# Both down-projection tiles of an expert in one transfer: neurons dealt by eights, up columns read in runs of 8

## The chip, the cores and the metric

The kernel runs on one core of one Trainium2 chip. The metric is the device time of one execution in microseconds, the median of three runs; a profiled execution has a time of its own and a trace.

## What is computed

One decoder layer on 512 tokens of width 1024: a mixing sub-layer (attention, not touched here), then a mixture of experts with 32 experts, of which each token takes four. The part that matters:

```
def clamped_swiglu(u):
    x_glu, x_lin = u[..., ::2], u[..., 1::2]
    x_glu = jnp.minimum(x_glu, SWIGLU_LIMIT)
    x_lin = jnp.clip(x_lin, -SWIGLU_LIMIT, SWIGLU_LIMIT)
    return x_glu * jax.nn.sigmoid(SWIGLU_ALPHA * x_glu) * (x_lin + 1)
...
    up = lax.ragged_dot(xs, w_up, group_sizes) + b_up[e_sorted]
    down = lax.ragged_dot(clamped_swiglu(up), w_down, group_sizes) + b_down[e_sorted]
    out = jnp.zeros_like(hf).at[tok].add(down * g_sorted[:, None].astype(down.dtype))
```

An expert's `w_up` is 1024 x 2048 float32 (8 MB), its `w_down` 1024 x 1024 (4 MB). Column 2n and 2n+1 of `w_up` are the two inputs of neuron n, and row n of `w_down` is its output. Any order of the 1024 neurons gives the same sum.

## The kernel before

After the attention (up to about 415 us) a router sorts the tokens by expert into chunks of 32 slots; in this input there are 80 chunks. An expert's weights stand in SBUF as six tiles of 2 MB: tiles 0 to 3 are `w_up` (by its rows), tiles 4 and 5 are `w_down`. There are two sets of six, `par` 1 and 0, so that one expert can be loaded while another is used. PE works through 42 parts, each a run of chunks of one expert; four parts make a cycle, with three experts loaded in each of the ten cycles (`N_CYC`), 30 in all. The first two experts are loaded ahead.

For a chunk, PE (`part`) goes through the up tiles in `UP_ORDER` with the 32 tokens as weights: for each tile and each half `y` of the neurons, 2 x 4 products of 256 columns (L2016), four side by side in the four column strips of the array (`out_of(y, g)`). A float32 product stands as two instructions in the trace, so a chunk has 128 of L2016. DVE and ACT make the gated activations of half `y` and DVE turns them in 32x32 blocks (`actT[:, y]`). Then PE waits for `actT_ready[y]` and for `tile_in[par][4 + y]` and makes the down products of tile 4 + y (L2036, 32 instructions a half). At the end of each half `tile_used[4 + y]` rises. ACT scales the result (L970), and POOL scatters it with an adding indirect DMA into `token_sums`; another indirect DMA of POOL (L710) gathers the rows of a later chunk.

Which neuron meets which partition is set by the turn in blocks: partition 32g+r of `actT[:, y]` holds four neurons. Before, `w_dn` deals them as n = 512y + 4p + k, so tile 4 is the upper half of the matrix and tile 5 the lower, each with 16 KB in one piece for a partition.

All weight transfers are issued by SP, in one queue and in program order. `load_expert` waits for each tile until the last chunk that reads it is done, then issues: tile 0, tile 1, tiles 2 and 3 in one transfer of 4 MB (32 KB for a partition), tile 4, tile 5.

```
                sp.wait_ge(tile_used[2], used)
                sp.wait_ge(tile_used[3], used)
...
                for n in (4, 5):
                    sp.wait_ge(tile_used[n], used)
                    if not par and n == 4:
                        load_bias(slot, e)
                    load_tile(n, par, e)
```

The biases are split by POOL into three bfloat16 parts early in the program (L641, L644), written to HBM, and read back per expert (`load_bias`); PE adds them with small selection matrices `bsel` (L2024, L2030).

Of the kernel before, what the change touches and what calls it, by code (L numbers as in the profile page):

```python
# [7 lines left out]
ALU = mybir.AluOpType  # L8
# [7 lines left out]
P = 128  # L16
SEQ = 512
D = 1024
# [84 lines left out]
def hybrid_layer(nc, a, out):  # L103
# [6 lines left out]
    w_up2 = a["w_up"][0].rearrange("e (p z j) n -> z p e (j n)", p=P, z=2)  # L110
    w_dn = a["w_down"][0].rearrange("e (y p g) n -> y p e (g n)", p=P, y=2)
    consts = nc.inline_tensor(shape_constants(), name="shape_table").ap()
# [10 lines left out]
    with ExitStack() as ctx:  # L123
# [120 lines left out]
        def const(at, n):  # L244
            return cf[:, at - C_KEEP:at - C_KEEP + n]
# [184 lines left out]
        TILE_H, TILE_2 = 0, 8  # L430
        BCONST, ONES = 17, 2
        GATE_PARTS = (4, 5, 10, 11)
# [7 lines left out]
        def _(sp):  # L440
# [80 lines left out]
            def load_bias(b4, e):  # L521
                src = bias_d[bass.ds(e, 1)] if not isinstance(e, int) else bias_d[e:e + 1]
                sp.dma_start(biasw[0:36, b4, :], src.rearrange("e r n -> (e r) n")).then_inc(biasw_in[b4], 16)
# [62 lines left out]
            def load_expert(q, done, par, slot):  # L586

                e = of_place(ORD, q, 0, N_EXP - 1)
                used = of_place(FIRST, done, 1, MAX_CH)
                if par:  # L590
                    load_bias(slot, e)
                for n in (0, 1):
# [3 lines that stand above are left out]
                sp.wait_ge(tile_used[3], used)  # L596
                sp.dma_start(take((6 * (1 - par) + 2) * TILE, 2 * TILE), w_up2[1][:, bass.ds(e, 1)].rearrange("p e n -> p (e n)"))\
                  .then_inc(tile_in[par][3], 16)
                for n in (4, 5):
                    sp.wait_ge(tile_used[n], used)  # L600
                    if not par and n == 4:
                        load_bias(slot, e)
                    load_tile(n, par, e)

# [23 lines left out]
        def _(pool):  # L628
# [8 lines left out]
            pool.wait_ge(bias_in, 32)  # L637
            pool.wait_ge(ev_dve, 4)
            for part in range(3):
                split = bias_b[:, part, :]  # L640
                pool.tensor_copy(split, bias_f).then_inc(bias_split, 1)  # L641
                pool.wait_ge(bias_split, 2 * part + 1)
                if part < 2:
                    pool.tensor_tensor(bias_f, bias_f, split, ALU.subtract).then_inc(bias_split, 1)  # L644
                    pool.wait_ge(bias_split, 2 * part + 2)
            for part in range(3):
# [17 lines left out]
            for i in range(NT):  # L664
                pool.memset(tokb[:, i, 1:2], -4.0 * P * (NT - 1 - i)).then_inc(bconst, 1)
            pool.tensor_scalar(bsel.rearrange("p y g s -> p (y g) s"), bc(const(C_I96, 12), 2, SLOTS),
                               const(C_THIRD, 1), None, ALU.is_equal).then_inc(bconst, 1)
            pool.wait_ge(bias_out, 96)
# [94 lines left out]
        def _(act_e):  # L763
# [32 lines left out]
            def proj_evac(n):  # L796
                for i in range(NT):
# [14 lines left out]
                    elif n == 1:  # L812
                        if i == 0:
                            act_e.wait_ge(bias_split, 5)
                        for dup in range(2):
# [743 lines left out]
        def _(pe):  # L1559
# [432 lines left out]
            ins.then_inc(gate_ps, 1)  # L1992
            def part(q, par, slot, loads, bias_loads, with_third):

# [7 lines left out]
                with pe.Fori(0, chunks) as j:  # L2002
                    c = first + j

                    def out_of(bank, g):
                        return ps[SLOTS * g:SLOTS * (g + 1), bank, 0:256]

                    pe.wait_ge(xgT_ready, c + 1)
                    for y, n in UP_ORDER:
                        if y == 0:  # L2010
                            place = 3 if n == 2 and with_third else n
                            pe.wait_ge(tile_in[par][place], loads + (32 if (par, place) == (0, 3) else 0))
                        for k in range(2):
                            for g in range(4):
                                at = y * D + 256 * g
                                ins = pe.matmul(out_of(y, g), xgT[:, 2 * n + k, :],  # L2016
                                                tiles[par][n][:, k, at:at + 256],
                                                start=(n == 0 and k == 0), stop=False)
                        if y:
                            ins.then_inc(tile_used[n], 1)  # L2020
                        if n == 3:
                            pe.wait_ge(biasw_in[slot], bias_loads)
                            for g in range(4):
                                ins = pe.matmul(out_of(y, g), bsel[:, y, g, :], biasw[:, slot, :],  # L2024
                                                start=False, stop=True)
                            ins.then_inc(up_ps[y], 1)
# [4 lines left out]
                    for y in range(2):  # L2031
                        pe.wait_ge(actT_ready[y], c + 1)
                        pe.wait_ge(tile_in[par][4 + y], loads)
                        for k in range(4):
# [47 lines left out]
```

## Time and profile before

| what | value |
|---|---|
| time, median of 3 runs (lowest, highest) | 1415.01 us (1412.33, 1415.05) |
| profiled execution: its time, its span | 1411.59 us, 1409.7 us |
| mean granted clock of PE | 0.985 |
| PE busy (matmuls) | 1284.7 us, 91% |
| DVE, ACT, POOL busy | 44%, 25%, 22% |
| DMA queue of SP (q1): 466.61 MB | 80.1% of 16 engines' time |
| chain that ended last | PE 61%, DMA 30%, of which 24% transfers of `in_w_down` |
| up products (L2016), down products (L2036) | 582.3 us, 302.5 us busy |

The first 415 us hold the attention and the router, the 970 us behind them the experts, and the last 20 us the sum of the token rows and the final norm. In the stretch of the experts both PE and the DMA engines are busy nearly always; a share of DMA of 1.00 means that all 16 engines have work throughout. In the timeline a value in brackets is how long the engine sat idle before the instruction, and what ended it. In the chain, a line "DMA" runs from the issue of a transfer to its landing, which includes its time behind others in the queue.

### The profile page before, as it was taken

To read this page: it belongs to the slowest core of one execution; us is meant where nothing else is said; L and a number is where in the kernel's file an instruction comes from. 1 tells how busy PE (TensorE), PEld (TensorE's weight loads), DVE (VectorE), ACT (ScalarE), POOL (GpSimd) and SP (SyncE) were. 2 spreads that over 40 slices of the span, in tenths; PEclk is the share of its full clock that TensorE was granted. 3 is DMA by queue.
4 is the path that set the end of the run, shared out by engine and by line. 5 is a ranking of instruction groups with operands and counts; after the bars stand their busy time and mean duration, and the time that the engine had idled before them with its cause. 6 is when DMAs were issued, how large, how long until landed. Compare 5 with 4: busy or idle time off the path is not lost.

```text
span 1409.7 us, 45665 instructions
## 1 busy us (share of the span) xinstructions
PE 1284.7 (91%) x18509; PEld 754.1 (53%) x18510; DVE 623.8 (44%) x1737; ACT 345.9 (25%) x868; POOL 312.0 (22%) x421
## 2 busy tenths in 40 slices
PE   6999998999989999978989967799999999998994
PEld 3464455665555555544555534455555555555552
DVE  2578537884563333432333323233333433332345
ACT  2110016783232222211222211122222222221222
POOL 0400003553002222211222211122222222222222
PEclk9999999999999999999999989999999999999998
DMA  9877404005699999999999999999989989999998
GB/s 352 279 263 276 167 0 180 2 2 215 249 386 379 400 415 420 425 424 418 419 420 410 418 427 428 421 415 412 420 339 421 388 343 400 421 425 429 409 424 319
DMA packets 66540, 484.96 MB, mean 344 GB/s; under 512 B 9770, under 2 KB 16738, under 8 KB 45764
## 3 DMA queue, kind: packets, MB, share of 16 engines
q1 hardware_dynamic: 58052, 466.61, 80.1%
q0 software_dynamic: 8144, 17.78, 4.8%
q8 instruction: 27, 0.44, 0.1%
q14 instruction: 13, 0.11, 0.0%
q10 hardware_dynamic: 304, 0.02, 0.0%
HBM read 468.83 MB, written 19.93 MB: 347 GB/s over the span
## 4 chain that ended last, share of the span: by engine, by line
PE 61%; DMA 30%; DVE 4%; issue 3%; ACT 1%; SPq 1%; DVEq 0%; POOL 0%; POOLq 0%; ACTq 0%
DMA arena<-in_w_down 24%; PE ps L2016 23%; PE ps L2036 13%; PE ps L1677 9%; PE ps L1909 4%; DMA token_sums<-arena 3%; PE ps L1805 2%; PE ps L1776 2%; PE ps L1839 2%; DMA arena<-in_w_in 1%; PE ps L1644 1%; DMA arena<-xn_rows,arena 1%; DMA arena<-token_numbers 1%; PE ps L2024 1%; ACT arena L970 0%
## 5 line engine op out<-in xcount | busy, mean ns | idle before, releaser
L2016 PE MATMUL ps<-arena 128*32 128x256 f32 x10240 | 582.3, 381 | 44.7 <-issue 29.0
L2016 PEld LDWEIGHTS ps<-arena 128*32 128x32 f32 x10240 | 341.3, 111 | 262.3 <-issue 52.1
L2036 PE MATMUL ps<-arena 128*32 128x256 f32 x5120 | 302.5, 387 | 36.8 <-DMA arena<-in_w_down 35.4
L1495 DVE TENSOR_SCALAR arena<-ps 128x128 f32<-128x128 f32 x160 | 46.6, 291 | 565.7 <-PE ps L2024 560.4
L2036 PEld LDWEIGHTS ps<-arena 128*32 128x32 f32 x5120 | 155.9, 111 | 160.6 <-issue 45.8
L970 ACT ACTIVATE arena<-ps,arena 32x256 f32<-32x256 f32 x316 | 147.4, 466 | 380.2 <-DMA token_sums<-arena 239.5
L710 POOL DMA_INDIRECT arena<-xn_rows,arena x82 | 85.5, 1042 | 409.6 <-DVE arena L1456 266.5
L702 POOL DMA_INDIRECT token_sums<-arena x80 | 110.9, 1386 | 221.3 <-ACT arena L970 218.4
L961 ACT ACTIVATE arena<-arena 128x128 f32<-128x128 f32 x160 | 49.5, 310 | 387.6 <-DVE arena L1495 387.5
L1677 PE MATMUL ps<-arena 128*128 128x512 f32 (+1 forms) x320 | 127.7, 555 | 0.0
L1677 PEld LDWEIGHTS ps<-arena 128*128 128x128 f32 x320 | 60.1, 190 | 60.8 <-issue 57.7
L685 POOL TENSOR_SCALAR arena<-arena 128x128 f32<-128x128 f32 (+3 forms) x48 | 51.7, 1083 | 121.3 <-DVE arena L1262 109.4
L1503 DVE STREAM_TRANSPOSE arena<-arena 128x128 f32<-128x128 f32 x160 | 67.2, 420 | 5.5
L1456 DVE STREAM_TRANSPOSE arena<-arena 128x256 f32<-128x256 f32 x81 | 52.7, 651 | 18.5 <-DMA arena<-xn_rows,arena 15.9
L852 ACT ACTIVATE arena<-arena 128x128 f32<-128x128 f32 (+3 forms) x96 | 52.9, 552 | 27.9 <-DVE arena L1240 27.8
L1909 PE MATMUL ps<-arena 128*128 128x512 f32 x128 | 56.4, 595 | 0.0
L1498 DVE SCALAR_TENSOR_TENSOR arena<-arena 128x128 f32<-128x128 f32 x160 | 46.9, 293 | 20.4
L750 POOL COPY arena<-arena 128x1 int32 x79 | 21.7, 275 | 149.5 <-DMA arena<-xn_rows,arena 149.2
L1501 DVE TENSOR_TENSOR arena<-arena 128x128 f32<-128x128 f32 x160 | 46.7, 292 | 6.3 <-ACT arena L961 0.8
L2024 PE MATMUL ps<-arena 128*32 128x256 bf16 x640 | 47.8, 274 | 0.0
L1055 DVE SCALAR_TENSOR_TENSOR arena<-arena 128x512 f32<-128x512 f32 x56 | 46.0, 821 | 2.0
L1240 DVE CUSTOM_DVE_ANT_0 arena<-ps,arena 128x128 f32<-128x128 f32 (+3 forms) x96 | 42.0, 484 | 6.6 <-PE ps L1776 6.6
(335 smaller groups left out, 951.3 us busy)
## 6 DMA issues: line engine op xcount, KB each, us to landing
arena<-in_w_up SPq DMA_DIRECT2D x67, 2048.0 KB, 14.0
arena<-in_w_down SPq DMA_DIRECT2D x64, 2048.0 KB, 28.5
arena<-in_w_up SPq DMA_DIRECT2D x30, 4096.0 KB, 26.6
arena<-in_w_ada SPq DMA_DIRECT2D x11, 2048.0 KB, 12.0
arena<-in_w_in SPq DMA_DIRECT2D x5, 2048.0 KB, 9.8
arena<-in_w_o SPq DMA_DIRECT2D x2, 2048.0 KB, 10.6
arena<-in_x SPq DMA_DIRECT2D x4, 512.0 KB, 5.0
arena<-in_w_ada SPq DMA_DIRECT2D x2, 1024.0 KB, 11.9
```

The lines of the kernel that those rows point to most:

```text
L685: ins = pool.tensor_scalar(pb, pb, scl[:, u % 4, 2 * n + 1:2 * n + 2], None, ALU.mult)
L702: pool.indirect_dma_start(sums, bass.IndirectOffsetOnAxis(idxs, 0), rows, None, bounds_check=SEQ - 1, oob_is_err=False, compute_op=ALU.add ...
L710: pool.indirect_dma_start(xg_in, None, xn2_d, bass.IndirectOffsetOnAxis(rows, 0), bounds_check=4 * SEQ - 1, oob_is_err=False).then_inc(gat ...
L852: ins = act_e.activation(pb, pb, ACT.Exp, scale=-1.0, bias=negm[:, n:n + 1], accum_out=lsum[:, n:n + 1])
L970: ins = act_e.activation(ybuf[:, 256 * g:256 * (g + 1)], ps[rows, 5, 0:256], ACT.Copy, scale=gate_all[rows, bass.ds(c, 1)])
L1456: v.transpose(turned, rows).then_inc(xg_turned, 1)
L1503: v.transpose(actT[:, y], act[:, y].rearrange("p (r g) -> p g r", g=4)).then_inc(actT_ready[y], 1)
L1677: ins = pe.matmul(ps[:, pj_bank(t), 0:width], hT[:, kt, i * P:(i + 1) * P], w[:, kt, :], start=(kt == 0), stop=(kt == KT - 1))
L1909: ins = pe.matmul(ps[:, t % 2 * 2 + grp, :], oT[:, kt, i * P:(i + 1) * P], wo[n][:, kt, :], start=(j == 0), stop=(j == 3))
L2016: ins = pe.matmul(out_of(y, g), xgT[:, 2 * n + k, :], tiles[par][n][:, k, at:at + 256], start=(n == 0 and k == 0), stop=False)
L2024: ins = pe.matmul(out_of(y, g), bsel[:, y, g, :], biasw[:, slot, :], start=False, stop=True)
L2036: ins = pe.matmul(out_of(5, g), actT[:, y, k, :], tiles[par][4 + y][:, k, 256 * g:256 * (g + 1)], start=False, stop=(y == 1 and k == 3))
```

## The change

Neurons are dealt as n = 8p + 4y + k. A partition's eight rows of `w_down` then lie side by side, 32 KB in one piece, and inside the loop tiles 4 and 5 come by one transfer of 4 MB, issued when both are free and announced on `tile_in[par][5]`; PE waits for that semaphore ahead of each of the two halves. The two transfers ahead of the loop stay two. In return the up columns of half y in strip g are no longer 256 neighbours but 32 runs of 8 out of 512 columns, and the biases of the up columns are split in the same order: what was one operation of 768 columns on POOL is now two of 256 in runs of 8 and one of 256. The selection matrix `bsel` is made by three operations, not one.

```
-    w_dn = a["w_down"][0].rearrange("e (y p g) n -> y p e (g n)", p=P, y=2)
+    w_dn = a["w_down"][0].rearrange("e (p y g) n -> y p e (g n)", p=P, y=2)
+    w_dn2 = a["w_down"][0].rearrange("e (p j) n -> p e (j n)", p=P)
...
-        BCONST, ONES = 17, 2
+        BCONST, ONES = 19, 2
...
-                for n in (4, 5):
-                    sp.wait_ge(tile_used[n], used)
-                    if not par and n == 4:
-                        load_bias(slot, e)
-                    load_tile(n, par, e)
+                sp.wait_ge(tile_used[4], used)
+                sp.wait_ge(tile_used[5], used)
+                if not par:
+                    load_bias(slot, e)
+                sp.dma_start(take((6 * (1 - par) + 4) * TILE, 2 * TILE), w_dn2[:, bass.ds(e, 1)].rearrange("p e n -> p (e n)"))\
+                  .then_inc(tile_in[par][5], 16)
...
+            up_f, down_f = bias_f[:, 0:512].rearrange("p (r y c) -> p y r c", y=2, c=8), bias_f[:, 512:768]
             for part in range(3):
-                split = bias_b[:, part, :]
-                pool.tensor_copy(split, bias_f).then_inc(bias_split, 1)
-                pool.wait_ge(bias_split, 2 * part + 1)
+                up_b = bias_b[:, part, 0:512].rearrange("p (y r c) -> p y r c", y=2, c=8)
+                down_b = bias_b[:, part, 512:768]
+                for y in range(2):
+                    pool.tensor_copy(up_b[:, y], up_f[:, y]).then_inc(bias_split, 1)
+                pool.tensor_copy(down_b, down_f).then_inc(bias_split, 1)
+                pool.wait_ge(bias_split, 6 * part + 3)
                 if part < 2:
-                    pool.tensor_tensor(bias_f, bias_f, split, ALU.subtract).then_inc(bias_split, 1)
-                    pool.wait_ge(bias_split, 2 * part + 2)
+                    for y in range(2):
+                        pool.tensor_tensor(up_f[:, y], up_f[:, y], up_b[:, y], ALU.subtract).then_inc(bias_split, 1)
+                    pool.tensor_tensor(down_f, down_f, down_b, ALU.subtract).then_inc(bias_split, 1)
+                    pool.wait_ge(bias_split, 6 * part + 6)
...
-                            act_e.wait_ge(bias_split, 5)
+                            act_e.wait_ge(bias_split, 15)
...
-            def part(q, par, slot, loads, bias_loads, with_third):
+            def part(q, par, slot, loads, bias_loads, in_pairs):
...
+                    def up_columns(row, y, g):
+                        return row[:, 512 * g:512 * g + 512].rearrange("p (r y c) -> p y r c", y=2, c=8)[:, y]
+
...
-                                at = y * D + 256 * g
-                                ins = pe.matmul(out_of(y, g), xgT[:, 2 * n + k, :],
-                                                tiles[par][n][:, k, at:at + 256],
+                                ins = pe.matmul(out_of(y, g), xgT[:, 2 * n + k, :], up_columns(tiles[par][n][:, k], y, g),
...
-                        pe.wait_ge(tile_in[par][4 + y], loads)
+                        pe.wait_ge(tile_in[par][5 if in_pairs else 4 + y], loads)
```

SP, one `load_expert` of `par` 1 inside the loop, before (an ISA row is a wait or a register instruction; `tile_used4` is the semaphore for tile 4):

```order
L518 ISA [waits tile_used0]
L518 DMA arena<-in_w_up 128x4096
L518 ISA [waits tile_used1]
L518 DMA arena<-in_w_up 128x4096
L597 ISA [waits tile_used3,tile_used2]
L597 DMA arena<-in_w_up 128x8192
L518 ISA [waits tile_used4]
L518 DMA arena<-in_w_down 128x4096
L518 ISA [waits tile_used5]
L518 DMA arena<-in_w_down 128x4096
```

And the same place of the changed kernel:

```order
L519 ISA [waits tile_used0]
L519 DMA arena<-in_w_up 128x4096
L519 ISA [waits tile_used1]
L519 DMA arena<-in_w_up 128x4096
L598 ISA [waits tile_used3,tile_used2]
L598 DMA arena<-in_w_up 128x8192
L604 ISA [waits tile_used5,tile_used4]
L604 DMA arena<-in_w_down 128x8192
```

The first of the two down transfers has moved behind the wait for tile 5 and has become one with the second.

PE, the end of a chunk of `par` 0 inside the loop, before (`tile_in04` is `tile_in[0][4]`):

```order
L2030 MATMUL ps<-arena 32x256 [waits y_ready]
L2030 MATMUL ps<-arena 32x256 x3
L2036 MATMUL ps<-arena 32x256 [waits tile_in04,actT_ready0]
L2036 MATMUL ps<-arena 32x256 x15
L2036 MATMUL ps<-arena 32x256 [waits tile_in05,actT_ready1]
L2036 MATMUL ps<-arena 32x256 x15
```

And of the changed kernel:

```order
L2041 MATMUL ps<-arena 32x256 [waits y_ready]
L2041 MATMUL ps<-arena 32x256 x3
L2047 MATMUL ps<-arena 32x256 [waits tile_in05,actT_ready0]
L2047 MATMUL ps<-arena 32x256 x15
L2047 MATMUL ps<-arena 32x256 [waits tile_in05,actT_ready1]
L2047 MATMUL ps<-arena 32x256 x15
```

No matmul is added or moved; the first down half now waits for the transfer for which only the second did.

## Rows read from the trace of the kernel before

**Rows 1.** Waits of PE, 430 to 1390 us: total us, times, longest.
```profile
PE ps L2036 <- DMA arena<-in_w_down: 35.4, 18, 3.5
```

**Rows 2.** Windows: us, busy (x) of PE, PEld, DVE, ACT, POOL, PEclk, DMA share, GB/s.
```profile
500.00:700.00 200.00, 180.81 (x3294) 106.69 (x3290) 69.78 (x208) 40.42 (x98) 45.07 (x65) 0.98 1.01 420
1026.00:1030.50 4.50, 4.50 (x84) 3.30 (x88) 0.00 (x0) 1.86 (x4) 1.24 (x2) 1.00 0.01 1
1126.50:1133.00 6.50, 5.36 (x104) 2.93 (x97) 2.21 (x6) 1.86 (x4) 1.75 (x3) 1.00 0.06 20
1180.00:1380.00 200.00, 187.29 (x3452) 110.33 (x3448) 74.30 (x221) 42.23 (x102) 46.69 (x68) 0.99 1.01 419
```

**Rows 3.** Chain that ended last: start us, us, what.
```profile
675.16 37.00 DMA arena<-in_w_down
...
991.70 34.15 DMA arena<-in_w_down
1061.48 33.30 DMA arena<-in_w_down
1256.36 37.11 DMA arena<-in_w_down
```

**Rows 4.** DMA issues in 1029:1031, then 772:773: KB, us to landing.
```profile
arena<-in_w_up SPq DMA_DIRECT2D x1, 2048.0 KB, 7.9
...
arena<-in_w_up SPq DMA_DIRECT2D x1, 2048.0 KB, 8.6
```

**Rows 5.** Timeline of PE: start us, us, instruction, [idle before <-releaser].
```profile
707.29 1.93 PE L2036 MATMUL ps<-arena 128*32 128x256 f32 x32 [1.15 <-DMA arena<-in_w_down]
712.29 1.94 PE L2036 MATMUL ps<-arena 128*32 128x256 f32 x32 [3.07 <-DMA arena<-in_w_down]
...
1022.45 1.93 PE L2036 MATMUL ps<-arena 128*32 128x256 f32 x32
1025.99 1.93 PE L2036 MATMUL ps<-arena 128*32 128x256 f32 x32 [1.60 <-DMA arena<-in_w_down]
...
1091.79 1.94 PE L2036 MATMUL ps<-arena 128*32 128x256 f32 x32
...
1293.61 2.71 PE L2036 MATMUL ps<-arena 128*32 128x256 f32 x32 [3.47 <-DMA arena<-in_w_down]
...
1384.16 1.93 PE L2036 MATMUL ps<-arena 128*32 128x256 f32 x32
1387.33 1.93 PE L2036 MATMUL ps<-arena 128*32 128x256 f32 x32 [1.24 <-DMA arena<-in_w_down]
```

**Rows 6.** DMA queue in 1105.5:1115, then 1116:1126: packets, MB, share of 16 engines.
```profile
q1 hardware_dynamic: 140, 3.64, 88.9%
...
q1 hardware_dynamic: 281, 3.31, 77.9%
```

**Rows 7.** Timeline of PE at two more waits.
```profile
618.70 3.62 PE L2036 MATMUL ps<-arena 128*32 128x256 f32 x32 [3.06 <-DMA arena<-in_w_down]
...
899.93 1.94 PE L2036 MATMUL ps<-arena 128*32 128x256 f32 x32 [2.99 <-DMA arena<-in_w_down]
```

**Rows 8.** Window behind the first of them, columns as in rows 2.
```profile
618.78:622.20 3.42, 3.42 (x36) 2.18 (x39) 0.00 (x0) 0.00 (x0) 0.00 (x0) 0.50 0.99 422
```

**Rows 9.** Weight loads up to 420 us: shapes xcount, busy us, mean ns, idle before.
```profile
L1882 PEld LDWEIGHTS ps<-arena 128*128 128x128 f32 x32 | 4.1, 190 | 2.2 <-issue 1.4 <-DVE arena L1366 0.7
L1625 PEld LDWEIGHTS ps<-arena 128*128 128x128 f32 x32 | 3.7, 140 | 2.7 <-DVE arena L1070 2.2 <-issue 0.5
```

**Rows 10.** Chain, 430 to 500 us: start us, us, what.
```profile
448.40 7.30 DMA token_sums<-arena
470.43 9.96 DMA token_sums<-arena
```

**Rows 11.** Timeline of POOL and of ACT: last bias split, first reader of its place.
```profile
57.29 1.17 POOL L641 CAST arena<-arena 128x768 bf16<-128x768 f32 x1
...
95.96 0.45 ACT L821 ACTIVATE arena<-ps 128x128 f32<-128x128 f32 x2 [4.82 <-PE ps L1677]
```

More of the change, by code:

```diff
@@ L665, in _ @@
                 pool.memset(tokb[:, i, 1:2], -4.0 * P * (NT - 1 - i)).then_inc(bconst, 1)
-            pool.tensor_scalar(bsel.rearrange("p y g s -> p (y g) s"), bc(const(C_I96, 12), 2, SLOTS),
-                               const(C_THIRD, 1), None, ALU.is_equal).then_inc(bconst, 1)
+            for y in range(3):
+                places = const(C_I96, 8)[:, y:8:2] if y < 2 else const(C_I96 + 8, 4)
+                pool.tensor_scalar(bsel[:, y], bc(places, 2, SLOTS), const(C_THIRD, 1), None, ALU.is_equal)\
+                    .then_inc(bconst, 1)
             pool.wait_ge(bias_out, 96)
@@ L2010, in part @@
                         if y == 0:
-                            place = 3 if n == 2 and with_third else n
+                            place = 3 if n == 2 and in_pairs else n
                             pe.wait_ge(tile_in[par][place], loads + (32 if (par, place) == (0, 3) else 0))
```

## The prediction

> **What bounds the kernel now.** I read the waits of PE first, because PE is busy 91% of the span. In the stretch of the experts it waits for `in_w_down` in 18 places, 35.4 us in total [rows 1]. Then I asked whether the transfers could come earlier, with a table of windows: from 500 to 700 us and from 1180 to 1380 us the DMA share is 1.01 [rows 2], so there the DMA engines have no time left and set the pace. But between 1026.0 and 1030.5 us the share is 0.01, and between 1126.5 and 1133.0 us 0.06 [rows 2]: the queue has run dry, because SP waits for PE to free a tile. So the two take turns. The chain of waits shows where one hands over to the other: transfers of `in_w_down` that land at 712.17, 1025.85, 1094.78 and 1293.48 us (start plus length) [rows 3], and each time PE goes on at once, 0.12 to 0.14 us later [rows 5]. The end is such a handover as well: the last down half starts at 1387.33 us after a wait for `in_w_down` [rows 5]. What the change does at these five places counts; elsewhere either the queue or PE has slack.
>
> One more view says how much slack. A transfer of 2 MB issued at 1029.85 us, into an empty queue, lands after 7.9 us; one issued at 772.5 us lands after 8.6 us [rows 4]. So at 772 us the queue was within 0.7 us of running dry, and what PE loses behind the landing at 712.17 us comes back as DMA idle time except for 0.7 us.
>
> **The first down half waits.** Before, the products of tile 4 (32 instructions, 1.93 us [rows 5]) lie in the shadow of tile 5's transfer: at 1022.45 us they run, and PE then idles until 1025.99 us [rows 5]. Now both halves start when the one transfer is there. A half takes 1.93 us alone, and 1.72 us to the start of what follows (712.29 to 714.01); I take 1.8 us. It is paid at each handover on the path: 1.1 us behind 712 us (1.8 less the slack of 0.7) and 1.8 us at 1025, 1094, 1293 and at the end, 8.3 us. At the other waits for `in_w_down` the queue is still full when PE next frees a tile, and the loss is absorbed; if all 18 [rows 1] counted, it would be 32 us, which is the outer bound of this term.
>
> Behind the waiting PE instruction stand the next chunk's up products, which are those that free tiles 0 and 1 for SP. That is how the loss returns to the queue. SP's own later issue of tile 4 costs nothing: it waits for tile 5's last product, one half later, and at that time 4 MB of tiles 2 and 3 are just issued ahead of it in the same queue.
>
> **The clock.** At these waits PE now idles in one piece. What such a wait does to the clock is shown by four of them in the trace, of nearly one length. At 618.70 us, after 3.06 us idle, the half takes 3.62 us, at 1293.61 us, after 3.47 us, 2.71 us; at 712.29 us, after 3.07 us, and at 899.93 us, after 2.99 us, it takes 1.94 us [rows 5, 7]. Behind the first the granted clock is 0.50 for 3.42 us, the lower of the two levels, 1.2 GHz [rows 8]. So a wait of this length costs 1.7 us in two of four cases (3.62 less 1.94). In the changed kernel the wait at 712 us would be about 5.9 us in one piece (1.15 + 1.93 + 3.07, less the overlap of the pipeline), longer than any of the four, so I count it in full, 1.7 us. At 1025 us it becomes 3.4 us (1022.45 to 1025.85), at 1094 us 3.0 us (1091.79 to 1094.78) and at the end 3.1 us (1384.16 to 1387.2): half of 1.7 us each, 2.6 us. At 1293 us the clock fell before, and nothing is added. That makes 4.3 us, bounds 0 and 6.8 us (four falls).
>
> **The transfer itself.** In 1105.5 to 1115 us nearly all packets of q1 are of tiles 2 and 3 (140 packets, 3.64 MB, 26 KB a packet): 88.9% of 9.5 us, 2.320 us a MB. In 1116 to 1126 us they are of the down tiles (281 packets, 3.31 MB, 12 KB a packet): 77.9% of 10 us, 2.353 us a MB [rows 6]. For 4.19 MB the longer pieces save 0.14 us. The queue is on the path, as above, while about 25 of the 30 experts are loaded (an estimate: all but those beside which it has run dry): 3.5 us. The lower bound is nothing. The upper one comes from the longest spacing of two landings of 2 MB in a full queue, about 5.4 us at 1288 to 1293 us (1.93 us of work and 3.47 us idle [rows 5]): 10.8 us for two, against 9.7 us for 4.19 MB at 2.320 us, 1.1 us an expert, 27 us in all.
>
> The Trainium skill ("SBUF — State Buffer", section "The DMA setup-cost knee") says that every transfer pays a roughly fixed 2 us, and asks to coalesce into the largest one; by that, 30 transfers fewer would give 60 us. The trace agrees that a lone transfer has such a cost, 7.9 us against about 5 us between landings (707.29 to 712.29 us), but in a full queue the next one's data moves meanwhile.
>
> **Up columns in runs of 8.** Nothing in the trace reads a moving operand in runs. The nearest rows are weight loads: with single words 32 bytes apart (L1882) one takes 190 ns, with words side by side (L1625) 140 ns, both 128 x 128 [rows 9]. That is 0.39 ns for each jump. Of 128 words in the first, each is alone in its 32 bytes; in the change eight stand together and fill 32 bytes. If only a short piece costs, the price is 0; if each jump does, it is 31 jumps x 0.39 = 12 ns an instruction, and with four strips side by side 10240 / 4 x 12 ns = 31 us of PE time. I take 0, since whole pieces of 32 bytes are read as before. The skill's same page (section "Door 1: The DMA port swizzle", on cachelines) says that reads are at full rate if a line of 16 bytes is hit at least twice; by that it is 0 as well.
>
> **Scatter beside larger pieces.** The scatter into `token_sums` took 7.30 us at 448.40 us, while tile 4 came, and 9.96 us at 470.43 us, while tiles 2 and 3 came [rows 10]. With the down tiles in 32 KB pieces more of them take the longer time. ACT and POOL hide it: the view of the waits names none of PE for ACT's L970; if that cover failed, it would be 2 to 3 us for each of the few chunks that follow one another without a DMA wait, up to 10 us. I take 0.
>
> **POOL's early work.** The bias splits end at 58.5 us, and the first to reuse their place is ACT at 95.96 us [rows 11]. Three operations in place of one, even at the full 1.17 us each, add about 12 us and leave 25 us. Nothing, as also for `bsel`.
>
> **Sum.** 8.3 + 4.3 - 3.5 = +9.1 us. On the profiled execution's 1411.6 us this is 1420.7 us; the median of the runs lies 3.4 us above the profiled one, which would make 1424.1 us. I say 1422 us, between the two.
>
> **Rivals.** (a) Faster, by one mechanism: a merged transfer saves more than its packets do. It decides from 0.5 us an expert on (12.6 us over 25 experts). At 0.67 us (two landings 5.2 us apart less 9.7 us) it gains 16.8 us and the kernel ends 4 us below before, 1409 us on the middle of the two bases. For it speaks the spacing of up to 5.4 us, against it the spacing of 5.00 us from 707.29 to 712.29 us, which leaves 0.27 us. Chance 0.12. Its extreme is that all of the difference between a lone transfer and the spacing in a full queue is saved, 7.9 - 5.0 = 2.9 us, 73 us for 25: 1351 us, chance 0.01, against which the full queue speaks. That extreme is what the skill's page on SBUF, named above, asks for. (b) No measurable change: the clock doesn't fall and the transfers save 0.3 us, 8.3 - 7.5 = +1 us, 1414 us. Chance 0.16. (c) The jumps cost PE time: 31 us over 80 chunks is 0.4 us a chunk. PE sets the pace in some 230 of the 970 us (the first 50, 712 to 775, 1026 to 1033, 1095 to 1169, 1293 to 1325), or 19 chunks, +8 us; as it slows, other stretches turn to it, up to the full 31 us. With +18 us on top it is 1440 us. Nothing speaks for it but the row of single words. Chance 0.08. (d) The scatter becomes what PE waits for: up to +10 us on top, 1431 us. For it speaks that ACT already waits for it in most chunks. Chance 0.08. The forecast itself, +3 to +16 us, has 0.55, its own range 1416 to 1430 us.
>
> **How the numbers follow.** A measurement of this kernel can tell about 0.2%, 2.8 us. Slower: the forecast, (c) and (d), 0.71. Within 0.2%: (b), 0.16. Faster: (a), 0.13. The range 1411 to 1433 us leaves out (a) for the most part and (c), 2 in 10.
>
> **What would show it.** In the changed profile: PE's waits for `in_w_down` at the first down half only, in pieces of 3 to 7 us, and more in total than 35.4 us by about 1.8 us for each; PE busy for the up products within 1% of 582.3 us (else (c)); gaps in the DMA share behind 1025 and 1126 us wider by 2 to 5 us; more stretches at clock 0.50 than before; q1's share lower by about 0.3 points for the same MB (if by over 1 point, (a)); and waits of PE for ACT's L970 or `y_ready` absent (else (d)). The prediction is wrong if the landings of `in_w_down` come earlier by more than PE loses behind them.

## The result and the profile after

The changed kernel takes 1427.8 us, the median of 6 runs (1426.2 to 1430.4); the kernel before, run beside it, takes 1415.03 us (6 runs, 1412.33 to 1417.54). The ratio is 1.0092, with a 95% interval of 1.0076 to 1.0109: slower by 12.8 us. The profiled execution took 1426.8 us, its span 1424.8 us, which is 15.1 us over the span of before. The profiled execution of before (1411.59 us) was shorter than all six that were counted, so the traces show 2.4 us more of a difference than the medians do.

The page of the changed kernel: engines, the DMA queue of the weights, the two groups of expert products (instructions | busy us, mean ns | idle before them and what ended it), and the transfers of the down tiles. L2028 and L2047 are the products that were L2016 and L2036.

```profile
PE 1295.4 (91%) x18509; PEld 758.9 (53%) x18510; DVE 621.5 (44%) x1737; ACT 346.0 (24%) x868; POOL 316.9 (22%) x433
...
q1 hardware_dynamic: 53732, 466.61, 79.1%
...
L2028 PE MATMUL ps<-arena 128*32 128x256 f32 x10240 | 580.4, 381 | 35.8 <-issue 28.8
...
L2047 PE MATMUL ps<-arena 128*32 128x256 f32 x5120 | 317.2, 402 | 48.1 <-DMA arena<-in_w_down 47.1
...
arena<-in_w_down SPq DMA_DIRECT2D x30, 4096.0 KB, 29.5
```

The number of MB is the same, in 4320 packets fewer, and the up products are as fast as before (580.4 against 582.3 us). The down products carry the loss: the idle time before them rose from 36.8 to 48.1 us, and the busy time of the same 5120 instructions from 302.5 to 317.2 us. Ahead of the up products PE sat idle less, 35.8 us in place of 44.7. Together that is 11.3 + 14.7 - 8.9 - 1.9 = 15.2 us. The waits of PE from 430 to 1405 us (total us, times, longest us), to be held against [rows 1]:

```profile
PE ps L2047 <- DMA arena<-in_w_down: 47.1, 12, 5.8
PE ps L2028 <- issue: 28.8, 40, 1.2
PE ps L2028 <- DMA arena<-in_w_up: 7.0, 1, 7.0
```

Instead of 18 waits of at most 3.5 us there are 12 of up to 5.8 us. The pieces at which a landing and the whole 64 products of the chunk follow one another, in the timeline of PE (start us, us, instruction, [idle before <-releaser]), against [rows 5, 7]:

```profile
902.03 6.27 PE L2047 MATMUL ps<-arena 128*32 128x256 f32 x64 [5.78 <-DMA arena<-in_w_down]
...
1032.20 3.66 PE L2047 MATMUL ps<-arena 128*32 128x256 f32 x64 [3.15 <-DMA arena<-in_w_down]
...
1102.82 6.57 PE L2047 MATMUL ps<-arena 128*32 128x256 f32 x64 [3.04 <-DMA arena<-in_w_down]
...
1305.88 5.74 PE L2047 MATMUL ps<-arena 128*32 128x256 f32 x64 [5.82 <-DMA arena<-in_w_down]
...
1400.87 3.66 PE L2047 MATMUL ps<-arena 128*32 128x256 f32 x64 [2.47 <-DMA arena<-in_w_down]
```

In [rows 5] the half behind the landing took 1.93 us where the clock held, since the other was done by then. Now both stand behind it: 3.66 us where the clock holds, 5.7 to 6.6 us where it doesn't. The windows behind four of the landings (columns as in [rows 2]), and the part from 707 us to the last landing as a whole:

```profile
712.80:716.20 3.40, 3.40 (x40) 2.17 (x36) 0.00 (x0) 0.00 (x0) 0.37 (x2) 0.50 0.99 423
900.50:907.30 6.80, 5.27 (x52) 2.94 (x56) 0.00 (x0) 0.00 (x0) 0.42 (x2) 0.50 1.01 427
1101.90:1108.70 6.80, 5.88 (x56) 3.22 (x60) 0.88 (x2) 0.00 (x0) 1.24 (x2) 0.50 1.01 429
1303.30:1310.10 6.80, 4.22 (x40) 2.24 (x44) 0.00 (x0) 0.00 (x0) 1.22 (x2) 0.50 1.00 421
...
707.00:1404.00 697.00, 635.82 (x11516) 374.82 (x11512) 249.55 (x745) 141.28 (x340) 159.38 (x225) 0.97 0.97 399
```

In the first four the granted clock is 0.50, the lower level, 1.2 GHz. The cost can be read off twice: half of the time that PE worked in the window (3.40, 5.27, 5.88, 4.22 us) is 1.7, 2.6, 2.9 and 2.1 us, and the products took 5.35, 6.27, 6.57 and 5.74 us against 3.66 us, 1.7, 2.6, 2.9 and 2.1 us more. Two windows of before belong beside them:

```profile
1294.62:1298.04 3.42, 3.42 (x40) 2.18 (x34) 0.00 (x0) 1.39 (x3) 0.00 (x0) 0.50 1.03 438
...
707.00:1390.00 683.00, 624.87 (x11488) 369.23 (x11488) 248.11 (x739) 140.62 (x338) 157.39 (x223) 0.99 0.99 408
```

The clock had fallen behind 1293 us before as well, for 1.7 us of PE's time: 0.8 us in the down half (2.71 less 1.93), the rest in the up products behind it. The two long windows say where the loss ends up: the DMA share is 0.97 of 697 us now and was 0.99 of 683 us. Both make 676 us of DMA work, with some 7 us idle before and 21 us now. The 14 us of difference are the loss. A share is rounded to a hundredth, which is 3.5 us either way here; shares of windows of 1 us, added up, give 673 us of work in both, with 9.7 and 24.2 us idle.

**The path, landing by landing.** The chain of waits of the changed kernel (start us, us, what) gives the landings as start plus length, against [rows 3]:

```profile
678.74 32.95 DMA arena<-in_w_down
...
858.23 43.66 DMA arena<-in_w_down
...
998.25 33.82 DMA arena<-in_w_down
...
1069.99 32.69 DMA arena<-in_w_down
...
1270.33 35.41 DMA arena<-in_w_down
```

The landing at 899.79 us of before is the end of this row of its chain:

```profile
851.78 48.01 DMA arena<-in_w_down
```

The last landing of each kernel does not stand on its chain. It is taken 0.13 us ahead of PE's start, as at the other places.

| landing before | after | later by | grown since the one above | products behind it, before → after | more |
|---|---|---|---|---|---|
| 712.17 | 711.69 | -0.5 | | 1.94 → 5.35 | 3.4 |
| 899.79 | 901.89 | 2.1 | 2.6 | 1.94 → 6.27 | 4.3 |
| 1025.85 | 1032.07 | 6.2 | 4.1 | 1.93 → 3.66 | 1.7 |
| 1094.78 | 1102.68 | 7.9 | 1.7 | 1.93 → 6.57 | 4.6 |
| 1293.48 | 1305.74 | 12.3 | 4.4 | 2.71 → 5.74 | 3.0 |
| 1387.2 | 1400.74 | 13.5 | 1.3 | 1.93 → 3.66 | 1.7 |

What the last column adds comes back as growth in the row below, but for 0.8 us behind the first row and 1.8 us behind 1293 us. About 0.9 us of the latter is no slack: before, the low clock went on into the up products, which this column does not count. Before rounding the column adds up to 18.9 us; 15.3 us arrive at the end of the last products (1389.26 to 1404.53 us), and the span grew by 15.1. There are six such places; the prediction had five. At the sixth, 899.8 us, the queue of before never ran dry afterwards, but it was near to it; now it runs dry there too, as the first of these windows of the changed kernel shows (DMA share 0.60; from 920 to 940 us of before none of the four windows of 5 us is under 1.00). The other two are the gaps that [rows 2] showed at 1026.0 and 1126.5 us:

```profile
930.00:935.00 5.00, 3.87 (x73) 2.46 (x76) 0.00 (x0) 1.86 (x4) 1.10 (x2) 1.00 0.60 192
1032.50:1038.00 5.50, 5.50 (x108) 4.02 (x104) 0.00 (x0) 1.79 (x4) 1.24 (x2) 1.00 0.01 1
1134.00:1146.00 12.00, 10.88 (x208) 6.26 (x204) 4.37 (x13) 4.11 (x10) 3.80 (x6) 1.00 0.12 22
```

In [rows 2] 4.5 us at share 0.01 and 6.5 us at 0.06 were shown; now it is 5.5 us at 0.01 and 12 us at 0.12.

One part of the chain misleads. From 1314.73 us on it runs over eight scatters into `token_sums`, where that of before ran over PE, as if the scatter had become the bound. The last products end 15.3 us later and the span is 15.1 us longer, so nothing was lost behind them, and in the view of waits PE has none for the scatter. I read it as two paths that came level at the end.

### The profile page after: what moved, and what is told of

It reads as the page before. It is cut to its first block, busy times and chain, and to the rows that moved or that the text cites. A ratio compares the mean times of both kernels' runs of the same rounds, so it can differ in the third digit from the quotient of the medians.

```text
span 1424.8 us, 45617 instructions
## 1 busy us (share of the span) xinstructions
PE 1295.4 (91%) x18509; PEld 758.9 (53%) x18510; DVE 621.5 (44%) x1737; ACT 346.0 (24%) x868; POOL 316.9 (22%) x433
## 3 DMA queue, kind: packets, MB, share of 16 engines
q1 hardware_dynamic: 53732, 466.61, 79.1%
## 4 chain that ended last, share of the span: by engine, by line
PE 61%; DMA 30%; DVE 4%; issue 3%; ACT 2%; SPq 0%; DVEq 0%; ACTq 0%; POOLq 0%; POOL 0%
DMA arena<-in_w_down 23%; PE ps L2028 21%; PE ps L2047 15%; PE ps L1687 9%; DMA token_sums<-arena 5%; PE ps L1919 4%; PE ps L1815 2%; PE ps L1786 2%; PE ps L1849 2%; PE ps L1654 1%; ACT arena L980 1%; DMA arena<-xn_rows,arena 1%; PE ps L2035 1%; PE ps L1666 0%; PE ps L1674 0%
## 5 line engine op out<-in xcount | busy, mean ns | idle before, releaser
L2028 PE MATMUL ps<-arena 128*32 128x256 f32 x10240 | 580.4, 381 | 35.8 <-issue 28.8
L2028 PEld LDWEIGHTS ps<-arena 128*32 128x32 f32 x10240 | 339.2, 111 | 252.9 <-issue 51.0
L2047 PE MATMUL ps<-arena 128*32 128x256 f32 x5120 | 317.2, 402 | 48.1 <-DMA arena<-in_w_down 47.1
L1505 DVE TENSOR_SCALAR arena<-ps 128x128 f32<-128x128 f32 x160 | 46.5, 291 | 577.2 <-PE ps L2035 571.7
L2047 PEld LDWEIGHTS ps<-arena 128*32 128x32 f32 x5120 | 164.5, 115 | 179.0 <-issue 69.9
L980 ACT ACTIVATE arena<-ps,arena 32x256 f32<-32x256 f32 x316 | 147.4, 466 | 457.6 <-DMA token_sums<-arena 333.9
L760 POOL COPY arena<-arena 128x1 int32 x79 | 25.5, 323 | 147.5 <-DMA arena<-xn_rows,arena 147.3
L1506 DVE TENSOR_SCALAR arena<-ps 128x128 f32<-128x128 f32 x160 | 44.9, 280 | 0.0
## 6 DMA issues: line engine op xcount, KB each, us to landing
arena<-in_w_up SPq DMA_DIRECT2D x67, 2048.0 KB, 15.7
```

The costliest lines, as they stand in the source:

```text
L980: ins = act_e.activation(ybuf[:, 256 * g:256 * (g + 1)], ps[rows, 5, 0:256], ACT.Copy, scale=gate_all[rows, bass.ds(c, 1)])
L2028: ins = pe.matmul(out_of(y, g), xgT[:, 2 * n + k, :], up_columns(tiles[par][n][:, k], y, g), start=(n == 0 and k == 0), stop=False)
L2047: ins = pe.matmul(out_of(5, g), actT[:, y, k, :], tiles[par][4 + y][:, k, 256 * g:256 * (g + 1)], start=False, stop=(y == 1 and k == 3))
```

## The experiments

Theory A: the loss is the wait. The first down half now stands behind the landing of the second, at every place where queue and PE hand over, with the clock falling behind the longer waits; the 4-MB transfer gives a little back, and the new deal of neurons with its runs of 8 costs nothing. Rival B: reading in runs of 8, or POOL's finer pieces, costs something. Rival C: it is the 4-MB transfer that hurts, by its size in the queue.

**The deal alone.** The changed kernel with two transfers of 2 MB, each waited for by its own half:

```
-                sp.wait_ge(tile_used[4], used)
-                sp.wait_ge(tile_used[5], used)
-                if not par:
-                    load_bias(slot, e)
-                sp.dma_start(take((6 * (1 - par) + 4) * TILE, 2 * TILE), w_dn2[...])
+                for n in (4, 5):
+                    sp.wait_ge(tile_used[n], used)
+                    if not par and n == 4:
+                        load_bias(slot, e)
+                    load_tile(n, par, e)
...
-                        pe.wait_ge(tile_in[par][5 if in_pairs else 4 + y], loads)
+                        pe.wait_ge(tile_in[par][4 + y], loads)
```

> The changed kernel with its new deal of neurons and its up columns in runs of 8, but tiles 4 and 5 again by two transfers of 2 MB, each with its own wait. Theory (PE gets the first down half too late, and its clock falls in the longer wait): the time goes back to that of the kernel before, 1412 to 1418 us, with 15 to 20 waits of PE for in_w_down of at most 3.5 us, in all about 35 us. Rival (the runs of 8 or the deal of the biases cost something): 1420 us or more, with the up products busier than 582 us. Rival (the pieces of 16 KB now 32 KB apart in HBM load more slowly): two landings of the down tiles lie more than 5.4 us apart on the mean, and the time lies above 1418 us.

Measured: 1417.51 us (12 runs) beside 1417.68 us, ratio 0.9998 (0.9988 to 1.0008). Waits of PE in this kernel, same columns as above:

```profile
PE ps L2046 <- DMA arena<-in_w_down: 35.6, 17, 3.4
```

This is [rows 1] again (35.4, 18, 3.5). B falls: deal, runs of 8 and POOL's pieces together are worth no more than 0.12% either way. Nor do pieces of 16 KB that lie 32 KB apart load more slowly: q1's time is 79.7% of 1416.8 us, 1129.2 us, as before.

This trace shows one thing more. At three of the six places the clock fell here too, behind waits as long as those of before:

```profile
713.91 3.64 PE L2046 MATMUL ps<-arena 128*32 128x256 f32 x32 [3.07 <-DMA arena<-in_w_down]
...
903.66 3.19 PE L2046 MATMUL ps<-arena 128*32 128x256 f32 x32 [3.06 <-DMA arena<-in_w_down]
...
1300.89 3.21 PE L2046 MATMUL ps<-arena 128*32 128x256 f32 x32 [3.37 <-DMA arena<-in_w_down]
```

So how often it falls differs from one execution to the next, and one pair of traces can't give its price. The mean granted clock of all executions can show that the change makes it fall more: it was 0.970 to 0.975 in the six of the changed kernel, 0.980 to 0.987 in the twelve of this one, and 0.979 to 0.987 in those of the kernel before beside them.

**The wait alone.** The kernel before, with its two transfers, but both halves waiting for the second:

```
-                        pe.wait_ge(tile_in[par][4 + y], loads)
+                        pe.wait_ge(tile_in[par][5], loads)
```

> The kernel before with one edit on PE alone: both down halves wait for tile 5; transfers, deal and columns are as before. Theory (the late first half and the clock are the whole loss, and the merged transfer gains 2 to 3 us): 1427 to 1432 us, at or a little above the changed kernel, with about 12 waits for in_w_down, the longest 5 to 6 us, and eight or more stretches at clock 0.50 in the experts' part. Rival (the loss comes from the transfer of 4 MB itself, by SP's later issue or by the slower scatter beside pieces of 32 KB): 1415 to 1419 us.

Measured: 1434.42 us (4 runs), ratio 1.0114 (1.0097 to 1.0131), 16 us slower. Its waits of PE, the down products on its page, and two of the handovers:

```profile
PE ps L2036 <- DMA arena<-in_w_down: 48.1, 11, 6.7
...
L2036 PE MATMUL ps<-arena 128*32 128x256 f32 x5120 | 313.7, 399 | 55.4 <-DMA arena<-in_w_down 51.0
...
1035.99 5.35 PE L2036 MATMUL ps<-arena 128*32 128x256 f32 x64 [3.28 <-DMA arena<-in_w_down]
...
1407.17 5.35 PE L2036 MATMUL ps<-arena 128*32 128x256 f32 x64 [2.84 <-DMA arena<-in_w_down]
```

The picture of the changed kernel (47.1, 12, 5.8; 317.2 us), without any transfer of 4 MB. The wait alone costs as much as the whole change or more (1.0114 against 1.0092, with intervals that overlap); C falls. That the 3 us between them are what the merged transfer gives back is not shown: here the clock fell at all six places, also at the two where it held in the changed kernel, and the six blocks of 64 products took 5.35, 5.96, 5.35, 4.98, 6.36 and 5.35 us, 2.1 us more in total than there. The time came out 2 us above what was expected, beside a kernel before of 1417.68 us in place of 1415.03. From 430 us to the last down product the granted clock was 0.50 in 10 stretches, as many as in the changed kernel, against 5 in the kernel before; its mean was 0.970 to 0.974 in the four executions.

**Less behind the last landing.** If the cost is the work that is left when the last bytes land, the kernel before should gain by leaving less. Its tile 5 came as 1 + 1 MB, then as 1.5 + 0.5 MB, and PE waited for the last piece only before the products that use it:

```
+                if n == 5:
+                    for half in range(2):
+                        cols = slice(half * TILE // 2, (half + 1) * TILE // 2)
+                        sp.dma_start(take(... + half * TILE // 2, TILE // 2), src[:, :, cols]...)\
+                          .then_inc((tile_in[par][5], last_in[par])[half], 16)
+                    return
...
                         for k in range(4):
+                            if y and k == 2:
+                                pe.wait_ge(last_in[par], loads)
```

> The kernel before with tile 5 loaded by two transfers of 1 MB (8 KB for a partition each); PE waits for the second ahead of the last quarter of the down products. Theory (what PE still has to do behind the landing of the last piece counts at each handover): 0.9 us less at each of some 6 handovers, and fewer falls of the clock, since the wait is cut again: 1406 to 1411 us. Rival (a transfer more costs 0.2 us or more of the queue's time, 30 times): 1413 us or more.

Measured: 1413.4 us (11 runs) beside 1417.68 us, ratio 0.9977 (0.9967 to 0.9986). The waits, and the products:

```profile
PE ps L2046 <- DMA arena<-in_w_down: 22.9, 24, 1.7
...
L2046 PE MATMUL ps<-arena 128*32 128x256 f32 x5120 | 299.1, 382 | 27.0 <-DMA arena<-in_w_down 22.9
```

The direction is right, but the time lies above the expected range, and where the rival had it (1413 us or more). The rival's mechanism isn't borne out: q1's time is 80.0% of 1410.9 us, 1128.7 us, no more than before (1129.2 us), so the added transfer cost the queue nothing that can be read. What did not come is the part on the clock: its mean over the executions is 0.983, as in the kernel before beside it. The waits for `in_w_down` fell by 12.5 us, but those for `in_w_up` grew from 15.7 to 21.9 us, so about half of what was gained at one wait moved to another.

> The kernel before with tile 5 loaded as 1.5 MB and 0.5 MB, PE waiting for the second ahead of the last eighth of the down products. Theory (what PE still has to do behind the last landing counts): 0.45 us less at each of some 6 handovers than with two times 1 MB, so 1409 to 1413 us where the kernel before takes 1417.7 us. Rival (pieces of 4 KB and the extra transfer cost the queue as much): equal to or above the version with two times 1 MB.

Measured: 1415.4 us (12 runs) beside 1418.47 us, ratio 0.9984 (0.9975 to 0.9993). The time lies above the expected 1409 to 1413 us, and the version is not better than the halves, as the rival had it; both intervals are below 1 and overlap. The waits for `in_w_down` hardly fall further (21.8 us). q1's time is 80.0% of 1415.0 us, 1132.0 us, about 3 us more than with the halves and as much as the expected gain (6 x 0.45 us). That fits the rival's reason, pieces of 4 KB that cost the queue time, but no run isolated it.

**A large transfer with a small one behind it.** The changed kernel with its 4 MB as 3 + 1 MB. PE starts the first half when 3 MB are there and waits for the last before the last quarter of the products:

```
-                sp.dma_start(take((6 * (1 - par) + 4) * TILE, 2 * TILE), w_dn2[...])\
-                  .then_inc(tile_in[par][5], 16)
+                for lo, hi, landed in ((0, 6, tile_in[par][5]), (6, 8, last_in[par])):
+                    sp.dma_start(take((6 * (1 - par) + 4) * TILE + lo * D, (hi - lo) * D),
+                                 w_dn2[:, bass.ds(e, 1), lo * D:hi * D]...).then_inc(landed, 16)
...
+                            if y and k == 2:
+                                pe.wait_ge(last_in[par], loads)
```

> The changed kernel with its 4 MB split as 3 MB (24 KB for a partition) and 1 MB (8 KB), the same count of transfers as before; PE starts its down products when the 3 MB are there, and waits for the last 1 MB ahead of the last quarter. The two transfers ahead of the loop have tile 5 in two halves. Theory: behind the last landing a quarter is left, 0.9 us in place of the changed kernel's 3.7 us, but the wait ahead of the first product is longer than in the kernel before (2.6 us more of transfer), so the clock falls more often than there: 1412 to 1419 us, 8 to 15 us below the changed kernel. Rival (a merged piece is bad in itself): it stays within 5 us of the changed kernel, above 1424 us.

Measured: 1414.49 us (12 runs) beside 1418.47 us, ratio 0.9971 (0.996 to 0.9982). Its waits of PE:

```profile
PE ps L2058 <- DMA arena<-in_w_down: 24.8, 12, 4.0
```

This beats both kernels: 0.29% below before, and with the changed kernel at 1.0092, 1.2% or 17 us below that (each held against the kernel before that ran beside it). From tile 5 as 1 + 1 MB (0.9977) it can't be told apart, so nothing shows a gain from merging the first three MB. It has the same deal and the same runs as the changed kernel, and inside the loop as many issues as the kernel before. Two things differ from the changed kernel: PE starts when 3 MB are there, and a quarter of the products stands behind the last landing.

**What short runs cost.** In the kernel before, the moving operand of the up products was read in single words 32 bytes apart, in runs of 4 words, and in runs of 2 words, each time as many words in all:

```
-                                at = y * D + 256 * g
...
-                                                tiles[par][n][:, k, at:at + 256],
+                                                tiles[par][n][:, k, y + 2 * g:2 * D:8],
```

> The kernel before, in which an up product reads 256 single words 32 bytes apart as its moving operand, over the whole row (so it multiplies other columns than it should; the rest is unchanged). If each jump costs what it costs a weight load, 0.39 ns, an instruction takes 100 ns more and the up products 256 us more in all, so that the kernel takes about 1650 us. If the moving operand can be read in single words for nothing, the time is that of the kernel before.

```
+                                                tiles[par][n][:, k, 512 * g:512 * g + 512].rearrange("p (r b c) -> p b r c", b=2, c=4)[:, y],
```

> The kernel before, in which an up product reads 64 runs of 4 words (16 bytes), 32 bytes apart, so it multiplies other columns than it should; the rest is unchanged. Single words cost 1978 us against 1418 us. If a read costs by pieces of 16 bytes touched, runs of 4 touch as many as words side by side, and the time is that of the kernel before. If each jump costs (1 ns, as for single words), 64 jumps make 64 ns an instruction and 160 us in all, about 1560 us.

> The same with 128 runs of 2 words (8 bytes), 16 bytes apart. By pieces of 16 bytes touched, twice as many as words side by side: if two words of a piece are enough for the full rate, the time is that of the kernel before; if each jump costs 1 ns, 128 ns an instruction and 320 us in all, about 1700 us.

Measured, single words: 1978.37 us (2 runs), ratio 1.3955. Runs of 4: 1417.7 us (8 runs), ratio 1.0004 (0.9991 to 1.0017). Runs of 2: 1423.87 us (4 runs), ratio 1.0041 (1.0022 to 1.006). The up products on the page of each of the three, one fence a kernel:

```profile
L2015 PE MATMUL ps<-arena 128*32 128x256 f32 x10240 | 1205.0, 640 | 30.2 <-issue 30.2
```

```profile
L2015 PE MATMUL ps<-arena 128*32 128x256 f32 x10240 | 585.2, 382 | 44.1 <-issue 29.0 <-DMA arena<-in_w_up 15.0
```

```profile
L2015 PE MATMUL ps<-arena 128*32 128x256 f32 x10240 | 611.4, 391 | 37.7 <-issue 29.3 <-DMA arena<-in_w_up 8.4
```

Against 582.3 us of before, runs of 4 words (16 bytes) are free, runs of 2 cost 29 us (5%), of which all but 6 us (ratio 1.0041) are hidden where the queue sets the pace, and single words more than double the time. The expectation for single words, about 1650 us, was a clear miss: it was worked out from the weight loads' 0.39 ns a word, and a word costs a moving operand 622.7 us / (2560 x 256) = 0.95 ns (2560 because four instructions run side by side). A row of weight loads bounded this cost badly.

## Why the prediction was right in sign and short in size

Predicted was 1422 us, slower with 0.71, the range 1411 to 1433 us; measured were 1427.8 us. On the profiled execution the sum was +9.1 us, and 15.2 us came (1411.59 to 1426.8 us); by the medians it is 12.8 us. One step makes most of the difference: a sixth place where queue and PE hand over, at 899.8 us, was taken for slack.

- **The first down half waits: right.** 1.7 us a handover (3.66 less 1.93) against the 1.8 us taken. At the predicted places it is as worked out, and with the sixth at 899.8 us, which the prediction lists as a wait but doesn't count as a handover, the term is 6 x 1.73 less the slack of 0.7, 9.7 us in place of 8.3. The step that failed is the claim that the loss at other waits "is absorbed": a wait of 2.99 us with a full queue behind it was taken for slack without a look at how near to dry the queue came. The place lost 4.3 us, and 4.1 us of them stand in the next landing. One transfer's time from issue to landing would have told: the one issued at 926 to 928 us in the kernel before took 9.8 us, against 7.9 us into an empty queue [rows 4], so not more than some 1.9 us were left to absorb 4.3.
- **The clock: the mechanism right, the term mis-sized.** Predicted 4.3 us with an upper bound of 6.8, measured 1.7 + 2.6 + 2.9 + 2.1, less the 1.7 that 1293 us had before (half of 3.42 us), 7.6 us. Of these the place left out, 899.8 us, has 2.6. The four places at which the prediction counted a fall have 4.6 in place of 4.3, in part by luck: it fell at two of them where 2.5 falls were counted, and the one at 1102 us cost 2.9 in place of 1.7. The place at 1293 us, for which nothing was added, lost 0.4 us more. The price of a fall was set too low: three of the four low stretches lasted 6.8 us, where the prediction took the one of 3.42 us [rows 8] for all, and with twice the products behind the landing the low clock finds more to slow. Whether it falls can't be told from the wait's length: it fell behind 3.04 us and held behind 3.15 us. At 712 us the wait was not the 5.9 us in one piece that the prediction worked out, but 3.33 us, and it fell all the same. The 7.6 us stand for this pair of traces alone: in the run with the deal alone the clock fell at three of the places, in the profile of before at one. No run here held the clock up through a wait to show its price apart.
- **The transfer: right that it is small, and smaller still.** q1's time is 79.1% of 1424.8 us, 1127.0 us, against 80.1% of 1409.7 us, 1129.2 us: 2.2 us over 30 experts, 0.07 us each where 0.14 us was taken (each of the two times is rounded to 0.7 us, so the 2.2 us are rough). The two terms make 9.7 + 7.6 = 17.3 us and 15.3 arrived. The 2.0 us left over are where a gain of the transfer would have to be, with whatever slack there was: the table has 0.5 us in the earlier landing at 712 us, 0.5 us in the three rows behind it and 0.9 us behind 1293 us. The Trainium skill ("SBUF — State Buffer", section "The DMA setup-cost knee") gives every transfer a fixed cost of about 2 us, an estimate of 60 us for the 30 transfers saved. The trace does not agree here: q1 worked 2.2 us less and the time rose. Behind other transfers in a full queue the size of one sets how much work stands behind its landing.
- **Runs of 8 free: right**, 580.4 us against 582.3 us, and the run with the deal alone agrees. Not by the reason given, though: the prediction spoke of whole pieces of 32 bytes, and runs of 16 bytes are free as well. The Trainium skill's rule (same page, section "Door 1: The DMA port swizzle") of two hits in a line of 16 bytes would have had runs of 8 bytes free too; the same place has each access that crosses to a new line pay a penalty, without a size. Measured, runs of 8 bytes cost 5%.
- **Scatter: right in cost, with thinner cover.** ACT's wait for `token_sums` (L970 before, L980 now) rose from 239.5 us in 50 waits to 333.9 us in 63. It goes with the transfer of 4 MB, not with the late first half: with the wait alone it is 233.3 us in 53 waits, and with 3 + 1 MB 219.7 us in 49. That each scatter takes longer beside the larger pieces is the likely reason and is not shown, since the times to landing of the scatters are not to be had in the trace of before. PE never waited for them.
- **POOL's splits: right.** They end at 62.5 us in place of 58.5 us, long before ACT's first use of their place [rows 11].
- **The marks named beforehand**: waits at the first half only, 10 of the 12 in pieces of 3 to 6 us and two shorter (2.06 and 2.47 us); the gaps behind 1025 and 1126 us wider, by 2.1 us of idle DMA time (0.61 of 1020 to 1035 us before, 0.47 of 1026 to 1041 us now) and 4.8 us (0.75 and 0.59 of 1120 to 1150 us); more stretches at 0.50, 10 in place of 5; up products within 1%: all seen. q1's share fell by 1.0 point, not 0.3, mostly because the span grew (1127.0 us are 79.9% of the old span). That mark was badly chosen: a share moves with its base, and the busy time is what to compare.

## What to carry to other kernels

Where a stream of transfers and its consumer take turns as the bound, what counts of a transfer is how much of the consumer's work lies behind its last byte. Cut the last piece small: 3 + 1 MB and 2 + 1 + 1 MB both beat both kernels here, and a last piece of 0.5 MB was no better. That merging what comes early gains anything was not shown. To find the places, don't stop at the waits on the chain: for each wait look whether the queue runs dry within the next transfers, and how close it comes (the time from issue to landing against that into an empty queue). Where the clock may fall behind a wait that grows, count the wait and, with a chance, half of PE's busy time in the stretch at 0.50. And compare falls of the clock over all executions: one profiled execution of before had one fall at the six places, and one of a kernel as fast had three.

## What the runs showed that was not expected

- The granted clock stayed at 0.50 for 3.4 us in some stretches and for 6.8 us in others, in the changed kernel and in the one that has only the wait. The kernel before had four of 3.4 us (one in [rows 8]) and one of 10.2 us, from 823.6 to 833.8 us, so the longer ones could have been seen beforehand.
- A moving operand of f32 reads at full rate in runs of 16 bytes with 16 bytes between them, at 5% less in runs of 8 bytes, and at 640 ns in place of 381 ns for 256 single words 32 bytes apart.
- Busy time of the down products depends on where they wait: 299.1 us with short waits, 302.5 us before, 313.7 and 317.2 us with long ones, always for the same 5120 instructions. The mean granted clocks of the four profiled executions go the same way: 0.986, 0.985, 0.974 and 0.973.
